# An mLSTM layer inside a long single-core program: decays folded into the queries, the read of the state summed in PSUM, and another order of the work around it

## The reference, cut to what matters

```python
    def step(carry, inp):
        c_prev, n_prev, m_prev = carry
        tot_c, m_l, c_l, n_l = inp
        m_new = jnp.maximum(tot_c + m_prev, m_l)
        a = jnp.exp(tot_c + m_prev - m_new)
        bb = jnp.exp(m_l - m_new)
        new = (a[..., None, None] * c_prev + bb[..., None, None] * c_l,
               a[..., None] * n_prev + bb[..., None] * n_l, m_new)
        return new, carry
    ...
    a_t = jnp.exp(inter - m_t)
    num = (jnp.einsum('bhcts,bhcsv->bhctv', s_qk, v)
           + a_t[..., None] * jnp.einsum('bhcvk,bhctk->bhctv', c_st, q))
    den = jnp.sum(s_qk, axis=-1) + a_t * jnp.einsum('bhck,bhctk->bhct', n_st, q)
    out = num / jnp.maximum(jnp.abs(den), jnp.exp(-m_t))[..., None]
```

## Time and profile before

| | us |
|---|---|
| median of 3 runs | 1559.55 (1559.46 to 1567.86) |
| profiled execution, its own time | 1564.55 |
| span of the profiled execution | 1562.7 |
| TensorE busy, share of the span | 1469.1 (94%) |
| VectorE busy | 993.5 (64%) |
| ScalarE busy | 754.6 (48%) |
| GpSimd busy | 67.5 (4%) |
| moved by DMA | 202.84 MB, mean 130 GB/s |

### The profile page before, as it was taken

How to read it: one execution, slowest core, us unless ns; L and a number is a source line. 1 busy time by engine, 2 the same in 40 slices (tenths; PEclk the granted TensorE clock), 3 DMA queues, 4 the chain that set the end, 5 groups by cost and what they waited for, 6 DMA issues and landing times.

```text
span 1562.7 us, 24142 instructions
## 1 busy us (share of the span) xinstructions
PE 1469.1 (94%) x9392; PEld 1204.4 (77%) x9392; DVE 993.5 (64%) x2286; ACT 754.6 (48%) x1630; POOL 67.5 (4%) x76
## 2 busy tenths in 40 slices
PE   6999999999999999999979999897999899999999
PEld 4777766777778777888757777576787798799987
DVE  4647677565566648535684677666777476777763
ACT  4436566453655443331143555555566347455542
POOL 0000000100000100020010100001101020000000
PEclk9999999999999999999989999899999999999999
DMA  9121180222560332221461253333435542445554
GB/s 362 55 108 55 57 316 21 102 82 67 189 230 1 108 102 81 94 68 54 170 221 54 76 159 102 139 98 126 162 125 155 197 161 95 149 148 189 189 189 135
DMA packets 59866, 202.84 MB, mean 130 GB/s; under 512 B 7694, under 2 KB 10984, under 8 KB 59624
## 3 DMA queue, kind: packets, MB, share of 16 engines
q1 hardware_dynamic: 53568, 192.84, 35.5%
q10 hardware_dynamic: 6008, 7.40, 2.1%
q0 software_dynamic: 176, 1.06, 0.2%
HBM read 199.43 MB, written 1.84 MB: 129 GB/s over the span
## 4 chain that ended last, share of the span: by engine, by line
PE 72%; DVE 15%; ACT 5%; DMA 4%; issue 3%; POOL 1%; SPq 0%; ACTq 0%; POOLq 0%; DVEq 0%
PE ps L2243 66%; PE ps L2246 5%; DVE w_l L2913 3%; DVE st L3012 1%; ACT w_h L2556 1%; DVE l_P L2917 1%; DVE x L2921 1%; DMA w_l_ada<-in_l_ada 1%; DMA w_raw<-in_l_out 1%; DVE m_P L3496 1%; ACT l_P L2559 1%; DVE l_xn L2917 1%; DVE l_h_lat L2921 1%; DMA w_raw<-in_l_ada 1%; POOL mstat L3590 1%
## 5 line engine op out<-in xcount | busy, mean ns | idle before, releaser
L2913 DVE TENSOR_TENSOR w_l<-w_raw,w_h 128x1024 fp32r<-128x1024 f32 (+3 forms) x263 | 315.4, 1206 | 74.9 <-ACT w_h L2556 74.4
L2556 ACT ACTIVATE w_h<-w_raw 128x1024 fp32r<-128x1024 f32 (+3 forms) x263 | 272.1, 1042 | 109.6 <-DMA w_raw<-in_f_down 25.3
L2243 PE MATMUL ps<-w_h,l_hTh 128*128 128x512 f32 (+1 forms) x384 | 156.2, 407 | 0.5 <-DVE w_l L2913 0.4
L2243 PE MATMUL ps<-w_h,l_hTl 128*128 128x512 f32 (+1 forms) x384 | 151.8, 395 | 0.0
L2243 PE MATMUL ps<-w_l,l_hTh 128*128 128x512 f32 (+1 forms) x384 | 151.8, 395 | 0.0
L2559 ACT ACTIVATE l_P<-ps,st 128x512 f32<-128x512 f32 (+1 forms) x128 | 77.6, 608 | 91.5 <-DVE st L2921 64.2
L3012 DVE TENSOR_REDUCE st<-ps 128x1 f32<-128x512 f32 (+2 forms) x112 | 72.7, 649 | 43.9 <-PE ps L2243 43.7
L2243 PE MATMUL ps<-f_hTh,w_h 128*128 128x256 f32 x352 | 99.2, 282 | 0.0
L2243 PE MATMUL ps<-f_hTl,w_h 128*128 128x256 f32 x352 | 99.1, 281 | 0.0
L2243 PE MATMUL ps<-f_hTh,w_l 128*128 128x256 f32 x352 | 99.0, 281 | 0.0
L2243 PE MATMUL ps<-l_hTh,w_h 128*128 128x512 f32 (+1 forms) x264 | 97.5, 369 | 0.5 <-issue 0.5
(11 more groups left out here) (444 smaller groups left out, 3467.9 us busy)
## 6 DMA issues: line engine op xcount, KB each, us to landing
w_raw<-in_l_ada SPq DMA_DIRECT2D x49, 512.0 KB, 5.3
w_raw<-in_l_z SPq DMA_DIRECT2D x32, 512.0 KB, 3.5
w_raw<-in_l_adg SPq DMA_DIRECT2D x32, 512.0 KB, 3.9
w_raw<-in_l_out SPq DMA_DIRECT2D x32, 512.0 KB, 4.7
w_raw<-in_m_merge SPq DMA_DIRECT2D x24, 512.0 KB, 3.3
w_raw<-in_f_gate SPq DMA_DIRECT2D x22, 512.0 KB, 3.3
w_raw<-in_f_up SPq DMA_DIRECT2D x22, 512.0 KB, 3.2
w_raw<-in_f_down SPq DMA_DIRECT2D x22, 512.0 KB, 4.2
```

The source lines that it names most:

```text
L2243: return p.e.matmul(out, lhsT, rhs, start=start, stop=stop)
L2556: return p.e.activation(out, a, func, scale=scale)
L2913: return p.e.tensor_tensor(out, a, b, op)
```

## The change

Four edits.

1. **Queries scaled.** Half of the decay `a` is written as an f32r pair of rows (`ar`: two ScalarE copies, two VectorE subtractions, in `ml_max`); the turn of `a` into columns goes. `ml_scaled(x)`: four f32r matmuls of 128 columns spread the decay over the partitions of a bank, and one VectorE product 128x512 writes the scaled queries `qa`. It runs at the second part of step x-2, for x = 2 to 7, between the rows' sums and the state matmuls. It reads `k0` or the queries' own place.
2. **One PSUM group.** The state is read with 257 columns into the same columns as the local sum, `start=False`. The 2-column matmuls, `ml_carried`, `ml_edge` and four small instructions of `ml_den` go; the denominators are copied behind all eight matmuls.
3. **Order.** Steps, `ada`, context finish and two steps of the latent finish (now tile 1 first) are woven anew: M1 to M7 with steps 4 and 5, M8 to M11 with step 6, M12 to the end with step 7; 7, 5 and 4 of the context finish's 16 steps beside them. The load of `gpost` waits for a fence and is issued with M10. `finish` takes each tile's `fin_o`, `fin_sq` and power together, and does `fin_rows` in two parts, heads 0 and 1 ahead of kp = 0, heads 2 and 3 ahead of kp = 2.
4. **Turn.** Blocks w0 to w2 are split before the turn, not w0 and w1. Four more steps of the latent finish (`fin_o`, `fin_sq` of tile 0 and the first part of both tiles' rows), then 5 context pieces, then the last 3 pieces woven with the remaining 10 steps.

```diff
-def weave(main, other, num, den):
+def along(main, other, num, den):
 ...
+        yield
     drain(other)
+
+def weave(main, other, num, den):
+    drain(along(main, other, num, den))
...
         if beside:
-            weave(beside, upto(half, 8), 8, 14)
+            drain(upto(beside, 4))
+            drain(upto(half, 5))
+            weave(beside, upto(half, 3), 3, 10)
...
-        gate, ctx = Gate(p, 2, *gate, f), m.finish(CTX, f, (2,))
-        mod = p.ada(PAIR, [(3, 0), (2, "gate"), (3, 1)], gate)
-        drain(braid(upto(steps, 6), upto(mod, 6), upto(ctx, 3)))
-        gate.free = p.fence()
-        drain(braid(steps, mod, ctx))
-        p.W.split_to(len(p.W.order) + 1, len(p.W.order) + 1)
+        ctx, lat = m.finish(CTX, lambda: f, (2,)), m.finish((1, 0), lambda: f, TRANS)
+        mod = p.ada(PAIR, [(3, 0), (2, "gate"), (3, 1)], Gate(p, 2, *gate, lambda: done))
+        weave(along(upto(steps, 6), upto(mod, 7), 7, 6), upto(ctx, 7), 7, 6)
+        done = p.fence()
+        weave(along(upto(steps, 3), upto(mod, 4), 4, 3), upto(ctx, 5), 5, 3)
+        weave(along(along(steps, mod, 7, 3), ctx, 2, 1), upto(lat, 2), 2, 3)
+        p.W.split_to(len(p.W.order) + 2, len(p.W.order) + 2)
         f = p.fence()
-        lat = m.finish(LAT, f, TRANS)
...
-            p.ml_local_mm(self, x, t, bo)
-            bd = p.take(pool) if c else None
-            p.ml_den(self, x, d, c, t, bo, bd, self.dn_tok.get((d, c - 1)))
-            if c:
-                p.give(bd, ("lstm", "last", x))
-            p.ml_carry_mm(self, x, d, c, t, bo)
+            p.ml_local_mm(self, x, d, c, t, bo)
+            p.ml_den(self, x, d, t, bo, self.dn_tok.get((d, c - 1)))
...
+            if x < 6:
+                scaled(x + 2)
...
         for t in pair:
             p.fin_o(self, t, [self.htok[t, h] for h in range(4)])
             yield
-        for t in pair:
             p.fin_sq(self, t)
-            yield
             p.rows_rstd4(self, t)
-        for t in pair:
-            p.fin_rows(self, t)
             yield
         for kp in range(4):
+            for t in pair if kp % 2 == 0 else ():
+                p.fin_rows(self, t, kp)
+                yield
...
+            y = p.mm(p.n.bank(bo[h], 257), m.Dt[x][:, h * 128:h * 128 + 128], m.va[:, t, h, :], True, c == 0)
...
         for h in range(4) if c else ():
-            p.wait_ge(("lstm", "den", x))
-            p.mm(p.n.bank(bo[h])[:, 257:512], m.qk[:, h, t * 128:t * 128 + 128], m.C[:, 4 * d + h, 0:255], True, True).then_inc(
-                *p.mark("lstm", "carry", x, h))
+            p.wait_ge(("lstm", "qa", x), ("lstm", "C", x - 2, h))
+            p.mm(p.n.bank(bo[h], 257), m.qa(x)[:, h], m.C[:, 4 * d + h, :], False, True).then_inc(*p.mark("lstm", "sum", x, h))
+
+    def ml_scaled(p, m, x, d, t, b, out):
+        s0 = slice(t % 2 * 128, t % 2 * 128 + 128)
+        p.wait_ge(("gates", "ar"), p.B.freed[b])
+        for h in range(4):
+            pick = m.pick[:, 4 * d + h:4 * d + h + 1].to_broadcast([128, 128])
+            y = p.mm(p.n.bank(b)[:, h * 128:h * 128 + 128], pick, m.ar[t // 2][:, s0], True, True)
+        y.then_inc(*p.mark("lstm", "spread", x))
...
+    def ml_scaled(p, m, x, d, t, b, out):
+        four = p.n.bank(b).rearrange("p (h t) -> p h t", h=4)
+        p.wait_ge(("lstm", "spread", x), ("lstm", "qk", t), ("lstm", "state", x - 4, 3) if x in (4, 5) else None)
+        p.tt(out, m.qk[:, 0:4, t * 128:t * 128 + 128], four, ALU.mult).then_inc(*p.mark("lstm", "qa", x))
```

More of the change, by code:

```diff
@@ L984, in next @@
         b.nsplit = self.split_n
+        s = b.j % NR
         if not raw:
@@ L1674, in chunks @@
         self.kE = lambda d, c: self.k0[d][:] if c == 0 else self.kt[:, self.ORDER[d][c], :]
+        rows = lambda t: self.qk[:, 0:4, t * 128:t * 128 + 128]
+        self.qa = lambda x: (self.k0[x - 4][:].rearrange("p (h t) -> p h t", h=4) if x in (4, 5) else
+                             rows(self.ORDER[steps[x][0]][steps[x][1]]))
         def exponents(x):
@@ L1689, in masked, with scaled @@
             p.ml_masked(self, x, d, c, self.ORDER[d][c], fence)
+        def scaled(x):
+            d, c = steps[x]
+            b = p.take(pool)
+            p.ml_scaled(self, x, d, self.ORDER[d][c], b, self.qa(x))
+            p.give(b, ("lstm", "qa", x))
         exponents(0)
@@ L1708, in chunks @@
             for h in range(4):
[L1709 to L1714, removed]
+                key = ("lstm", "h", x, h)
+                p.ml_local(self, x, d, t, h, bo[h], fresh, self.htok.get((t, h)))
                 self.htok[t, h] = key
                 p.give(bo[h], key)
[L1717 to L1721, removed]
+            self.dn_tok[d, c] = ("lstm", "h", x, 3)
+            if x < 6:
+                scaled(x + 2)
             bc = []
@@ L2713, in ml_max @@
         p.f(r["a"][:], r["a"][:], ACT.Exp).then_inc(*p.mark("gates", "a"))
+        p.wait_ge(("gates", "a"), p.stage_tok)
+        for x in range(2):
+            y = p.copy(m.ar[x][0:64], r["a"][:, 256 * x:256 * x + 256], scale=0.5)
+        y.then_inc(*p.mark("gates", "ah"))
         p.wait_ge(("gates", "nm_in"))
@@ L3178, in ml_max @@
         p.tt(m.negMr[64:128], m.negM[:], m.negMr[0:64].bitcast(F32), ALU.subtract).then_inc(*p.mark("gates", "M"))
+        p.wait_ge(("gates", "ah"))
+        for x in range(2):
+            y = p.stt(m.ar[x][64:128], r["a"][:, 256 * x:256 * x + 256], 0.5, m.ar[x][0:64].bitcast(F32), ALU.mult, ALU.subtract)
+        y.then_inc(*p.mark("gates", "ar"))
     def ml_cols(p, m, b, fence):
@@ L3227, in ml_masked, with ml_den @@
         p.tt(D[:], D[:], m.ST[:, t, :], ALU.mult).then_inc(*p.mark("lstm", "D", x))
[L3229 to L3232 removed]
+    def ml_scaled(p, m, x, d, t, b, out):
+        four = p.n.bank(b).rearrange("p (h t) -> p h t", h=4)
+        p.wait_ge(("lstm", "spread", x), ("lstm", "qk", t), ("lstm", "state", x - 4, 3) if x in (4, 5) else None)
+        p.tt(out, m.qk[:, 0:4, t * 128:t * 128 + 128], four, ALU.mult).then_inc(*p.mark("lstm", "qa", x))
+    def ml_den(p, m, x, d, t, bo, prev):
+        n, dn = p.n, m.dn[:, d]
+        p.wait_ge(("lstm", "sum", x, 3), prev)
         for h in range(4):
@@ L3246, in ml_den, with ml_local @@
         p.e.reciprocal(dn[:, 1], dn[:, 1]).then_inc(*p.mark("lstm", "recip", x))
-        if c:
-            p.wait_ge(("lstm", "recip", x))
-            p.stt(dn[:, 2], dn[:, 1], 0.5, a, ALU.mult, ALU.mult).then_inc(*p.mark("lstm", "gain", x))
-            p.wait_ge(("lstm", "gain", x))
-            p.tt(dn[:, 3], two[:, :, 0], dn[:, 2], ALU.mult).then_inc(*p.mark("lstm", "last", x))
-    def ml_local(p, m, x, d, c, t, h, b, fresh, old):
+    def ml_local(p, m, x, d, t, h, b, fresh, old):
         dst, src = m.h[t][:, h * 256:h * 256 + 256], p.n.bank(b, 256)
-        p.wait_ge(("lstm", "last" if c else "recip", x), ("lstm", "carry", x, h) if c else None)
+        p.wait_ge(("lstm", "recip", x))
         if fresh:
@@ L3294, in rows_rstd4, with fin_rows @@
         p.ts(s[:, 4:8], s[:, 0:4], 1.0 / 1024, ALU.mult, EPS, ALU.add).then_inc(*p.mark("fin", "mean", t))
-    def fin_rows(p, m, t):
+    def fin_rows(p, m, t, h0):
         s = p.n.st[:, 16 * t:16 * t + 16]
-        for h in range(4):
+        for h in (h0, h0 + 1):
             sl = slice(h * 256, h * 256 + 256)
```

57 lines of the change are left out of this document (17 added, 40 removed).

## The result

The change makes the kernel slower: 1572.75 us (median of 5 runs, 1569.67 to 1577.31), against 1559.55 us before (5 runs, 1554.47 to 1567.86). The ratio is 1.0081, 95% interval 1.0058 to 1.0104, so about 12.6 us. It lies outside the predicted range (1547 to 1568).

What follows compares the result with a forecast made beforehand. TensorE was taken as full in the z-projection, with room for an order to win between it and the out-projection. Spreads +0.5, gate rows +0.3, later stage about +0.2: 1559.55 + 1.0 = 1560.5 us, range 1547 to 1568.

Steps and rivals of the forecast that it cites:

- Through steps 4 and 5 the order is nearly the old one; M6 is where it was.: Steps 4 and 5: order taken as nearly unchanged, with M7 then coming ahead of step 6's eight matmuls, about 783.4.
- Step 7 behind M11, waiting for DMA: Ahead of step 7: M11 needs blocks a20 and a21, so step 7's local matmuls start at 796.3, not 791.27.
- From step 7 to the first piece: Step 7 to out-projection: VectorE's queue runs 11.5 us without a gap, 1 more for squares; first piece about 809.9.
- Piece 4 waits for w_l3, queued behind the latent finish: Out-projection: w_l3 stands on VectorE behind four latent finish steps, 6.2 us, so piece 4 waits until 820.6.
- The pieces: After piece 4: five pieces and four turns 8.4 us, low clock 2, turn 2 2.4; reaching 833.4, before 832.8.
- Gate rows: Beside the q and k projection: two ScalarE copies and two VectorE subtractions, at most 2.8 us, taken as 0.3.
- Spreads: TensorE's four f32r matmuls of 128 columns a step: 0.6 us, bounds 0.3 and 0.76; +0.5 us in the z-projection.
- A: Rival at the out-projection: the cover works, pieces start at 803.5 and run on; -12 us, 1547.5; chance 0.25.
- B: Rival at step 7 and later pieces: the DMA wait brings the clock down; +8 us, 1568; chance 0.20.
- C: Rival: the order neither helps nor hurts, only TensorE's work counts; -2.3 us, 1557.3; inside the forecast's 0.50.
- D: Rival in the steps: TensorE's exponents wait behind the scaled product; +3.6 us if not hidden; inside the forecast's 0.50.

Runs made afterwards that it cites:

- e5: The change with mean and power of a tile's squares put one finish step later; 1.0047 of the kernel before.
- e9: The change with late gate rows, late means, step 7's first part ahead of M10 and M11, and four blocks split; 0.9985 of the kernel before, 1558.58 us.
- e6: e5 with M10 and M11 behind step 7's first part instead of ahead of it; 1.0023 of the kernel before.
- e7: e5 with the fourth out-projection block, w3, split ahead of the turn too; 1.0021 of the kernel before.
- e4: e1 with the decay pair's two copies and two subtractions moved to a later piece of the preparation; 0.9993 of the kernel before.
- e1: The kernel before with edits 1 and 2 only, so new arithmetic in the old order; 1.0005 of the kernel before.
- e2: The kernel before with edits 3 and 4 only, so new order on the old arithmetic; 1.0127 of the kernel before.
- e12: e2 with late means, step 7's first part ahead of M10, and four blocks split; 1.0034 of the kernel before.

## Why the prediction was wrong

The forecast was +1.0 us, the result +12.6, by a mechanism of which the prediction had one half (the DMA ahead of step 7, piece 4 behind the latent finish) and missed the other. By the steps of the prediction:

- **"Through steps 4 and 5 the order is nearly the old one; M6 is where it was." This step failed**, and it holds most of the miss. It looked at where the mod steps stand and left out where edit 3's new form of `finish` puts the mean. Predicted for step 7's start: 796.3 - 760.06 = 36.2 us behind step 4's. Measured 42.7, so 6.4 us late. e5 moves the means alone, and its step 7 starts 36.8 us behind step 4: the forecast of 36.2 stands once they are out of the way. The working did price this same construction later on, at the latent rows ("1 more for the squares of tile 1", "ScalarE's four squares"), but not for the context tiles, whose finish has the same form. It also passed over the first context turn, which edit 3 draws in ahead of step 6 and for which TensorE waits 2.17 us; in e5 and e9 that wait is still there (2.24).
- **Step 7 behind M11, waiting for DMA: right in kind.** TensorE waits 1.73 us on `in_l_ada` directly ahead of step 7 (row at 805.23), and e6, which takes M10 and M11 away from there, gives back 6.4 us of stretch. The wait is later than forecast by what steps 5 and 6 had lost, and these did not give the DMA a lead: a load is issued when a block has been used, so TensorE's gaps held the loads back too (DMA share 0.19 from 783 to 786 us, in the last section).
- **From step 7 to the first piece:** predicted 809.9 - 796.3 = 13.6 us, measured 14.6.
- **Piece 4 waits for w_l3, queued behind the latent finish: right.** Predicted 10.7 us behind the first piece, measured 831.35 - 820.36 = 11.0. The profile names ScalarE's `w_h`, since its third rounding is the last event; VectorE's timeline has the cause:

```profile
827.77 0.17 DVE L2928 TENSOR_SCALAR st<-st 128x4 f32<-128x4 f32 x1 [1.77 <-ACT l_o L2565]
827.85 0.87 DVE L2931 SCALAR_TENSOR_TENSOR l_h_lat<-l_h_lat,st,l_z 128x256 f32<-128x256 f32 x2
829.23 0.88 DVE L2931 SCALAR_TENSOR_TENSOR l_h_lat<-l_h_lat,st,l_z 128x256 f32<-128x256 f32 x2 [0.50 <-POOL st L3588]
830.03 2.35 DVE L2923 TENSOR_TENSOR w_l<-w_raw,w_h 128x1024 fp32r<-128x1024 f32 x2
```

  Squares, mean, power, rows, `w_l3`, as the working had them; the first `w_l` ends at 831.2. ScalarE was late as well: it rounds w3 only at 827.65, behind the squares. e7 splits it ahead and gives 4.6 us back.
- **The pieces:** predicted 833.4 - 809.9 = 23.5 us to the first latent piece, measured 26.0, at a granted clock of 0.79 from 820.3 to 846.3 where the working had 2 us for it. Turn 2 waited 2.13 and 0.47 us for a predicted 2.4.
- **Gate rows: mis-sized**, +0.3 against 1.5 us. The bound of 2.8 held. The chosen value rested on "TensorE has dense matmuls queued", but these need a `w_l` of the same VectorE queue, and a subtraction that waits 1.05 us for ScalarE holds it up. e4 confirms it.
- **Spreads: mis-sized.** Three of the four in the z-projection start 0.39 or 0.40 us ahead of the next row, one (at 733.95) 0.61, for a predicted 0.6 each:

```profile
706.10 0.56 PE L2250 MATMUL ps<-l_arc,l_pick 128*128 128x128 f32 x4
706.49 1.74 PE L2250 MATMUL ps<-l_va,l_k 128*128 128x257 f32 x7
```

  What the 2-column matmuls took stands beside it, in a step of the z-projection before (8 of 2 and 8 of 255 columns) and after (8 of 257), each with the row behind:

```profile
725.47 2.78 PE L2243 MATMUL ps<-l_C,l_qk 128*128 128x2 f32 x16
727.90 0.58 PE L2243 MATMUL ps<-w_h,l_hTh 128*128 128x512 f32 x1
...
729.42 1.90 PE L2250 MATMUL ps<-l_C,l_qk 128*128 128x257 f32 x8
730.97 0.58 PE L2250 MATMUL ps<-w_h,l_hTh 128*128 128x512 f32 x1
```

  2.43 us against 1.55, so 0.88 for a predicted 0.94. The z-projection then comes to 1.79 - 2 x 0.88 = 0.0 us for the predicted +0.5; measured 0.0. The 0.2 us a step that the prediction worked out from the Trainium skill, "TensorE: Matmul & The Clock Gate", section Back-to-back issue gap, would make it 1.79 - 0.4 = +1.4. The figure of 60 cycles was misapplied there: the section gives its table for an isolated matmul and says that at small widths it counts too little, since it leaves out the weight load.
- **Sum.** 6.4 + 1.0 + 2.5 beyond the working, and its own 0.6, make 10.5 us, and 83.2 - 72.7 = 10.5. To this come 1.5 at the gate rows: 12.0, against the 12.6 of the ratio.

**The rivals.** A (the cover works) did not come: VectorE was not free by 803. Nor did any run reach its condition, pieces from 803.5, which is 43.4 us behind step 4: the earliest is 48.8 (e1, e6), e9 has 49.1 for 50.5 before. Its direction is there in e9, where the stretch is 5.8 us shorter, about half of its 12, and the time not clearly so. B (+8, through the clock) came nearest to the number: the clock does fall in step 6. But the place and the releaser were other ones, VectorE in step 5 and the turn ahead of step 6, and step 7, behind the DMA wait, ran at full clock (2.01 us). C (only the work counts) put -3.1 us on the stage from step 4 on and 0.8 ahead of it. For the arithmetic alone e1 has -2.3 there and 1.5 at the gate rows, so -0.8 for -2.3. D (exponents waiting behind the scaled product) has no such wait in the list. The new arithmetic does bring a smaller one nearby: in step 4 the state matmuls wait 1.06 us for the row sums (row at 769.42; e1, e4 and e9 have it too), where it was 0.29; step 5 still follows step 4 by 12.1 us for 12.5. That VectorE has 2 us less to do in a step was given a price only inside A; e2 against the change, and e12 against e9, show some 7 us where the order makes VectorE late. So edits 1 and 2 hid about a third of what edits 3 and 4 cost (e2: 19.8 us).

**Slips in the sums, on which nothing rests.** The opening's 7.7 us do not follow from the line that they stand in: in steps 4 to 7 TensorE idles 40.6 - 38.99 = 1.6 us; with the busy time lost to the lower clock, 6.09 x 0.36 + 17.89 x 0.22 = 6.1, it makes 7.7. And B's +8 on top of 1560.5 is 1568.5, not 1568.

## What to carry to other kernels

When an order is merged from several generators, list for each in-order engine what stands directly behind every instruction that waits for another engine; a 128x4 mean in front of row sums cost more here than all the arithmetic saved under the old order, and what it waited for was itself held up by a copy ahead of it in ScalarE's queue. Walk each changed form through every place that uses it, not only through the one that the change is about. And weigh less work on an engine only together with the order: it was worth 1 us at most where that engine had slack and some 7 where it was late.

## What the runs showed of the hardware

The granted clock did not follow the length of the last gap alone. In the change, gap and what follows (stretches of TensorE; the last three columns are the granted clock, the share of the DMA and GB/s):

```profile
780.50:783.00 2.50, 0.32 (x2) 0.30 (x2) 0.97 (x4) 1.49 (x8) 0.72 (x1) 1.00 0.94 334
783.00:786.00 3.00, 3.00 (x11) 2.35 (x9) 1.35 (x3) 0.00 (x0) 0.29 (x1) 0.58 0.19 74
...
790.00:793.00 3.00, 0.83 (x12) 0.45 (x5) 2.64 (x7) 0.00 (x0) 0.00 (x0) 1.00 1.01 333
793.00:798.00 5.00, 5.00 (x18) 4.09 (x16) 0.00 (x0) 0.00 (x0) 0.00 (x0) 0.66 0.89 350
```

and in e9:

```profile
785.50:788.00 2.50, 0.30 (x5) 0.10 (x1) 2.48 (x6) 0.00 (x0) 0.00 (x0) 1.00 0.81 277
788.00:792.00 4.00, 3.97 (x21) 3.24 (x21) 0.00 (x0) 0.84 (x2) 0.00 (x0) 1.00 0.99 387
```

A gap of 2.18 us in step 5 and one of 2.17 ahead of step 6 were each followed by 3 to 5 us at a mean of 0.58 and 0.66, that is mostly the lower level of 1.2 GHz; a gap of 2.24 us in e9, ahead of the same step 6, by none. e5 has the same picture as e9. What decides between them was not tried and stays open. It matters for the size: of the change's 6.7 us between step 4 and the first piece, the eight matmuls at 782.73 and the sixteen from 793.08 cost about 0.8 us more than step 4's eight (769.42) and 1.7 more than the same sixteen in e9 (to the next row 2.46 us for 1.68, and 5.25 for 3.57).
